# MLP down: the low halves of A21 and A21+A22 from a negative high half by ScalarE and an addition by DMA inside SBUF

## The chip, the cores and the metric

The kernel is one program on 1 core of a Trainium2 chip. The time is the device time of one execution in microseconds (us); a median stands for several runs. The profile is of one execution. Its engines are TensorE (PE, with its weight loads PEld), VectorE (DVE), ScalarE (ACT), GpSimd (POOL) and SyncE (SP). DMAs are issued from the queues of SP, ACT and POOL and moved by 16 DMA engines.

## The reference

Two transformer blocks in float32 on 512 tokens of width 1024. The first is attention with a gated convolution and an MLP; the second has two layers, retention and then chunk attention, each followed by an MLP with a squared ReLU. The change touches only that last MLP, which runs twice:

```python
def _sqrelu_mlp(h, w1, w2):
    u = jax.nn.relu(h @ w1)
    return (u * u) @ w2

for i in range(DEPTH_2):
    ...
    h = h + _sqrelu_mlp(_rmsnorm(h, mlp_norm_g[i]), mlp_w1[i], mlp_w2[i])
```

h is 512x1024, w1 is 1024x4096 and w2 is 4096x1024.

## The kernel before

**Three products for one.** Each float32 operand is split in a high half, rounded to fp32r by ScalarE, and a low half, the operand less the high one. `three` (L1043) multiplies high by high, high by low and low by high. So for each block of weights somebody has to make `w_hi` and then `w_lo`. In the MLPs ScalarE makes the first (`hi_of`, L1756) and VectorE the second (`lo_of`, L3258). GpSimd makes the low halves of most other stages (`lo`, L924).

**The MLP.** It goes in four groups of 1024 hidden columns, `MLP_GROUPS`. In each group the up products come first (units), then seven down products. The down product is a 2x2 block product with seven multiplications, from sums of blocks, in the order A11, A12, S3, M, A21, S1, S4 (`PRODUCTS`, L1516). S1 is A21+A22: its weights are loaded to `raw` and the second block is added by a DMA from HBM (L1016). S3, M and S4 share one buffer, `s3_m_s4` in `aux`: S3 is made by a load and an adding DMA (L1012), M by VectorE, which adds A21 (`m_sum`, L3302), and S4 by a further adding DMA (L1018) once M's low half is made. The hidden blocks are summed in the same way by VectorE: T3, T2, T4 (for A21), T1 (for S1).

**Places.** Every product needs two halves of weights, 128x1024 each. A half is a place (`down`, L174); `w_hi` and `w_lo` have four half slots each, so a half may be written when TensorE is through with the place four before (`released`, L194). Progress is counted in semaphores: `w_hi_ready` by ScalarE, `w_lo_ready` by whoever makes the low half, in the order of the places, `group_done` by TensorE. SyncE loads the next raw weights on `w_lo_ready` (`raw_free`, L220): A21's second half frees the slot of the next group's first weights, S1's that of the second.

**Order around the change.** Each engine runs its list as written. ScalarE: part T4's high half, A21's two high halves, T1's, S1's two, S4's two (L2459 to L2465). VectorE: T4's sum, `take` of a finished product from PSUM, T4's low half, two low halves of A21, T1's sum, a take, T1's low half, two of S1, a take, two of S4, then the takes of Q4 and Q5 (L3477 to L3496). S4 goes into the same PSUM banks as S1, and both results are wanted, S1's alone and the two together, so TensorE waits before each tile of S4 until VectorE has taken Q5 from that tile (L1586). GpSimd: the sums of units, then S3's, S1's and S4's adding DMAs (L1006 to L1018).

Of the kernel before, what the change touches and what calls it, by code (L numbers as in the profile page):

```python
# [348 lines left out]
SEMAPHORES = """first_in0 first_in1 first_in2 first_in3 first_hi rows_in pos_in ident_in kr_in ext_in ext_out bias_in0  # L349
 bias_in1 bias_in2 bias_in3 decay_in tab_in krep_done out_done raw_ready0 raw_ready1 w_hi_ready w_lo_ready group_done  # L350
# [14 lines left out]
def build(nc, T, out):  # L365
# [3 lines left out]
    with ExitStack() as ctx:  # L369
# [359 lines left out]
        def _(sp):  # L729
# [166 lines left out]
            for t in range(4):  # L896
# [850 lines left out]
        def _(act):  # L1747
# [35 lines left out]
            def down_hi(ml, g, b, half):  # L1783
# [536 lines left out]
            def mlp(ml, norm, turned, name, row):  # L2320
# [28 lines left out]
                def plain_squared(m):  # L2349
# [1432 lines left out]
```

## Time and profile before

| | us |
|---|---|
| median of 3 runs | 1985.72 (1985.52 to 1986.9) |
| the profiled execution | 1985.98 |
| its span, first to last instruction | 1984.1 |
| TensorE busy | 1932.1 (97%) |
| VectorE busy | 1324.9 (67%) |
| ScalarE busy | 978.0 (49%) |
| GpSimd busy | 643.7 (32%) |

The mean granted clock of TensorE is 0.994 of full speed. The page gives averages over very different stages; the timeline of one down stage tells more. In a timeline row the first number is the start in us from the span's start, the second the time from the first start to the last end of the merged instructions; a bracket gives the idle time before it and what ended it. Matmuls overlap, so their distance is read from start to start.

### The profile page before, as it was taken

To read this page: it belongs to the slowest core of one execution; us is meant where nothing else is said; L and a number is where in the kernel's file an instruction comes from. 1 tells how busy PE (TensorE), PEld (TensorE's weight loads), DVE (VectorE), ACT (ScalarE), POOL (GpSimd) and SP (SyncE) were. 2 spreads that over 40 slices of the span, in tenths; PEclk is the share of its full clock that TensorE was granted. 3 is DMA by queue.
4 is the path that set the end of the run, shared out by engine and by line. 5 is a ranking of instruction groups with operands and counts; after the bars stand their busy time and mean duration, and the time that the engine had idled before them with its cause. 6 is when DMAs were issued, how large, how long until landed. Compare 5 with 4: busy or idle time off the path is not lost.

```text
span 1984.1 us, 25953 instructions
## 1 busy us (share of the span) xinstructions
PE 1932.1 (97%) x10236; PEld 1643.6 (83%) x10236; DVE 1324.9 (67%) x1807; ACT 978.0 (49%) x1392; POOL 643.7 (32%) x456
## 2 busy tenths in 40 slices
PE   8999999999999999999998999999999998999997
PEld 6877878888888888888887798988888888798896
DVE  7667753432257845454557888889566777888888
ACT  7445442322245442424356564656455556564655
POOL 2333545555455435353542011110333341101010
PEclk9999999999999999999998999999999998999999
DMA  5312367375322322222223556565322233746554
GB/s 162 93 44 75 113 88 122 99 101 115 100 91 85 112 80 93 77 94 75 95 74 106 149 149 170 129 190 135 99 85 84 84 111 81 191 118 188 123 157 127
DMA packets 166220, 221.46 MB, mean 112 GB/s; under 512 B 4512, under 2 KB 119968, under 8 KB 165984
## 3 DMA queue, kind: packets, MB, share of 16 engines
q1 hardware_dynamic: 151600, 190.52, 29.6%
q0 software_dynamic: 12928, 25.71, 7.6%
q10 hardware_dynamic: 1584, 3.74, 4.2%
q8 instruction: 74, 1.21, 0.3%
q14 instruction: 34, 0.28, 0.0%
HBM read 214.84 MB, written 4.72 MB: 111 GB/s over the span
## 4 chain that ended last, share of the span: by engine, by line
PE 65%; DVE 19%; ACT 8%; issue 7%; POOL 1%; DMA 0%; SPq 0%; DVEq 0%; ACTq 0%; POOLq 0%
PE ps L1045 20%; PE ps L1047 20%; PE ps L1046 20%; DVE w_lo L3261 6%; DVE hid_lo L3276 2%; DVE o_buf L3399 2%; ACT w_hi L1759 2%; ACT x L2371 1%; PE ps L1217 1%; PE ps L1247 1%; ACT x L2373 1%; POOL w_lo L929 1%; DVE x L3356 1%; PE ps L1256 1%; ACT hid_hi L2385 1%
## 5 line engine op out<-in xcount | busy, mean ns | idle before, releaser
L929 POOL TENSOR_TENSOR w_lo<-raw,w_hi 128x512 fp32r<-128x512 f32 x376 | 531.8, 1445 | 665.3 <-ACT w_hi L1753 665.3
L1045 PE MATMUL ps<-hn_hi,w_hi 128*128 128x512 f32 (+1 forms) x1524 | 556.5, 365 | 2.2 <-DVE hn_lo L2961 1.7
L1047 PE MATMUL ps<-hn_hi,w_lo 128*128 128x512 f32 (+1 forms) x1524 | 547.7, 359 | 0.0
L1046 PE MATMUL ps<-hn_lo,w_hi 128*128 128x512 f32 (+1 forms) x1524 | 547.6, 359 | 0.0
L1045 PEld LDWEIGHTS ps<-hn_hi,w_hi 128*128 128x128 f32 x1524 | 289.4, 190 | 49.3 <-issue 3.8
L1753 ACT ACTIVATE w_hi<-raw 128x2048 fp32r<-128x2048 f32 (+1 forms) x98 | 186.0, 1898 | 287.1 <-PE ps L1047 287.0
L1047 PEld LDWEIGHTS ps<-hn_hi,w_lo 128*128 128x128 f32 x1524 | 288.8, 190 | 43.1
L1046 PEld LDWEIGHTS ps<-hn_lo,w_hi 128*128 128x128 f32 x1524 | 289.2, 190 | 41.9 <-issue 1.7
L1045 PE MATMUL ps<-w_hi,hid_hi 128*128 128x512 f32 x456 | 180.9, 397 | 22.4 <-issue 9.1
L1046 PE MATMUL ps<-hid_lo,w_hi 128*128 128x512 f32 (+1 forms) x504 | 184.3, 366 | 0.0
L1045 PE MATMUL ps<-hid_hi,w_hi 128*128 128x512 f32 (+1 forms) x488 | 179.5, 368 | 0.0
L1047 PE MATMUL ps<-hid_hi,w_lo 128*128 128x512 f32 (+1 forms) x488 | 178.1, 365 | 0.0
L1047 PE MATMUL ps<-w_hi,hid_lo 128*128 128x512 f32 x456 | 177.8, 390 | 0.0
L1046 PE MATMUL ps<-w_lo,hid_hi 128*128 128x512 f32 x456 | 177.5, 389 | 0.0
L1045 PEld LDWEIGHTS ps<-w_hi,hid_hi 128*128 128x128 f32 x456 | 85.5, 188 | 52.5 <-issue 35.6
L1759 ACT ACTIVATE w_hi<-raw 128x1024 fp32r<-128x1024 f32 x100 | 101.7, 1050 | 51.1 <-PE ps L1047 51.1
L2665 DVE TENSOR_TENSOR scr<-ps,scr 128x512 f32<-128x512 f32 x42 | 27.1, 686 | 138.7 <-PE ps L1047 135.3
L3261 DVE TENSOR_TENSOR w_lo<-raw,w_hi 128x1024 fp32r<-128x1024 f32 x92 | 110.8, 1222 | 7.7 <-ACT w_hi L1759 7.7
L1046 PEld LDWEIGHTS ps<-hid_lo,w_hi 128*128 128x128 f32 x504 | 95.1, 189 | 15.2 <-issue 0.2
L1045 PEld LDWEIGHTS ps<-hid_hi,w_hi 128*128 128x128 f32 x488 | 92.0, 189 | 16.8 <-DVE hid_lo L3061 0.8
L1047 PEld LDWEIGHTS ps<-hid_hi,w_lo 128*128 128x128 f32 x488 | 92.1, 189 | 14.8
L1047 PEld LDWEIGHTS ps<-w_hi,hid_lo 128*128 128x128 f32 x456 | 85.6, 188 | 18.5
(396 smaller groups left out, 3438.6 us busy)
## 6 DMA issues: line engine op xcount, KB each, us to landing
raw<-in_mlp_w SPq DMA_DIRECT2D x50, 1024.0 KB, 5.4
raw<-in_ret_w_in SPq DMA_DIRECT2D x24, 1024.0 KB, 5.1
aux<-in_mlp_w POOLq DMA_DIRECT2D x16, 1024.0 KB, 8.5
unit_raw<-in_mlp_w SPq DMA_DIRECT2D x14, 1024.0 KB, 6.4
raw<-in_att_w_in SPq DMA_DIRECT2D x12, 1024.0 KB, 5.4
raw<-in_w_gate SPq DMA_DIRECT2D x11, 1024.0 KB, 5.3
raw<-in_w_up SPq DMA_DIRECT2D x11, 1024.0 KB, 5.4
raw<-in_w_down SPq DMA_DIRECT2D x8, 1024.0 KB, 8.1
```

Source lines behind the costliest of these rows:

```text
L929: ins = pool.tensor_tensor(w_lo[:, slot, at], raw[:, slot, at], w_hi[:, slot, at].bitcast(F32), ALU.subtract)
L1045: pe.matmul(o, hi, rhs_hi, start=start, stop=False, skip_group_check=True)
L1046: pe.matmul(o, hi, rhs_lo, start=False, stop=False, skip_group_check=True)
L1047: return pe.matmul(o, lo, rhs_hi, start=False, stop=stop, skip_group_check=True)
L1217: ins = pe.matmul(a.score_ps(b, t), q[:, t * P:(t + 1) * P], k[:, 0:(t + 1) * P], start=(n == 0), stop=(n == last), skip_group_check=True)
L1247: ins = pe.transpose(a.trans_ps(b, j)[:, (t - j) * P:(t - j + 1) * P], a.score_sb(b, t)[:, j * P:(j + 1) * P], ident[:, :])
L1753: act.activation(w_hi[:, c.slot, 0:columns], raw[:, c.slot, 0:columns], ACT.Copy)\
L1759: act.activation(half_slot(w_hi, ml, place), src, ACT.Copy).then_inc(s["w_hi_ready"], ml.step(place))
L2665: dve.tensor_tensor(dst, ps[:, g.bank(m), :], r, ALU.mult).then_inc(pair_free[g.pair], 1)
L3261: dve.tensor_tensor(half_slot(w_lo, ml, place), src, half_slot(w_hi, ml, place).bitcast(F32), ALU.subtract)\
L3276: dve.tensor_tensor(lo_part, p_block(block), hi_part.bitcast(F32), ALU.subtract).then_inc(s["mlp_lo"], 1)
L3399: ins = dve.scalar_tensor_tensor(o, ps[:, bank + n, :], r_two[:, at:at + 1], o, ALU.mult, ALU.add)
```

## The change

In every group of both MLPs the four low halves of A21 and S1 are made otherwise. ScalarE writes the negative of the rounded block to the slot in `w_lo`, then the high half to `w_hi` as before. GpSimd issues a DMA from `raw` to `w_lo` with addition, which leaves raw less high. When it has landed GpSimd counts `w_lo_ready` up. VectorE drops these four subtractions and waits for S1's before it makes S4's. Several semaphores are put together: `m_summed` goes into `mlp_sum`, `out_done` and `ext_out` into `rows_out`.

```diff
+    BY_DMA = (A21, S1)
...
+    def by_dma(self, g, b):
+
+        return (2 * (self.first + g) + self.BY_DMA.index(b) + 1) * 16
...
     def first_sums(self, n):
-        return 20 * self.layer + n
+        return 28 * self.layer + n
 
     def sums(self, g, n):
-        return 20 * self.layer + 4 + 4 * g + n
+        return 28 * self.layer + 4 + 6 * g + n
...
-SUM = {T3: 1, T2: 2, T4: 3, T1: 4}
+SUM = {T3: 1, T2: 2, T4: 5, T1: 6}
+FIRST_SUM = {T3: 1, T2: 2, T4: 3, T1: 4}
+M_HALF = (3, 4)
...
+            def low_added(ml, g, b):
+
+                for half, landed in enumerate(("lo_first_in", "lo_second_in")):
+                    place = ml.down(g, b, half)
+                    pool.wait_ge(s["w_hi_ready"], ml.ready(place))
+                    pool.dma_start(half_slot(w_lo, ml, place), down_source(ml, g, b, half), accum_op=ALU.add)\
+                        .then_inc(s[landed], 16)
+
+            def low_landed(ml, g, b):
+
+                for half, landed in enumerate(("lo_first_in", "lo_second_in")):
+                    pool.wait_ge(s[landed], ml.by_dma(g, b))
+                    pool.nop().then_inc(s["w_lo_ready"], 1)
+
...
                     pool.dma_start(s1, w2[g, 0, 1], accum_op=ALU.add).then_inc(s["s1_added"], 16)
+                    low_added(ml, g, ml.A21)
                     pool.wait_ge(s["w_lo_ready"], ml.ready(ml.down(g, ml.M, 1)))
                     pool.dma_start(s3, w2[g, 0, 0], accum_op=ALU.add).then_inc(s["s4_added"], 16)
+                    low_landed(ml, g, ml.A21)
+                    low_added(ml, g, ml.S1)
+                    low_landed(ml, g, ml.S1)
...
+                if b in ml.BY_DMA:
+                    place = ml.down(g, b, half)
+                    act.wait_ge(s["group_done"], ml.released(place))
+                    act.activation(half_slot(w_lo, ml, place), down_source(ml, g, b, half), ACT.Copy, scale=-1.0)
                 hi_of(ml, ml.down(g, b, half), down_source(ml, g, b, half))
...
                     part_lo(g, T4)
-                    down_lo(g, ml.A21, 0)
-                    down_lo(g, ml.A21, 1)
                     t1(g)
                     take(g, ml.Q6, ml.M, 1, 1, 0, X, ALU.subtract)
                     part_lo(g, T1)
-                    down_lo(g, ml.S1, 0)
-                    down_lo(g, ml.S1, 1)
                     take(g, ml.Q2, ml.A11, 1, 0, 0, Z, ALU.add)
+                    dve.wait_ge(s["w_lo_ready"], ml.ready(ml.down(g, ml.S1, 1)))
                     down_lo(g, ml.S4, 0)
```

Three places of the order of instructions show it, all of group 1 of the first MLP but for GpSimd's, which are of group 0; the groups are alike. In the names, the tile written stands before the arrow. Lines of the changed kernel are some 7 to 29 higher.

ScalarE before, from M's high halves to S4's (L1759 makes a high half, L2385 that of a hidden part):

```order
L1759 ACTIVATE w_hi<-aux 128x1024 [waits group_done,m_summed] x2
L2385 ACTIVATE hid_hi<-x 128x1024 [waits mlp_sum]
L1759 ACTIVATE w_hi<-raw 128x1024 [waits group_done,raw_ready0] x2
L2385 ACTIVATE hid_hi<-x 128x1024 [waits mlp_sum]
L1759 ACTIVATE w_hi<-raw 128x1024 [waits group_done,s1_added] x2
L1759 ACTIVATE w_hi<-aux 128x1024 [waits group_done,s4_added] x2
```

and in the change (L1784 and L2414 are these two, L1824 the negative copy):

```order
L1784 ACTIVATE w_hi<-aux 128x1024 [waits group_done,mlp_sum] x2
L2414 ACTIVATE hid_hi<-x 128x1024 [waits mlp_sum]
L1824 ACTIVATE w_lo<-raw 128x1024 [waits group_done,raw_ready0]
L1784 ACTIVATE w_hi<-raw 128x1024 [waits group_done]
L1824 ACTIVATE w_lo<-raw 128x1024 [waits group_done,raw_ready0]
L1784 ACTIVATE w_hi<-raw 128x1024 [waits group_done]
L2414 ACTIVATE hid_hi<-x 128x1024 [waits mlp_sum]
L1824 ACTIVATE w_lo<-raw 128x1024 [waits group_done,s1_added]
L1784 ACTIVATE w_hi<-raw 128x1024 [waits group_done]
L1824 ACTIVATE w_lo<-raw 128x1024 [waits group_done,s1_added]
L1784 ACTIVATE w_hi<-raw 128x1024 [waits group_done]
L1784 ACTIVATE w_hi<-aux 128x1024 [waits group_done,s4_added] x2
```

Each high half of A21 and S1 has a negative copy in front of it, and T4's and T1's high halves (`hid_hi`) stand where they stood.

GpSimd before: the adding DMAs to S3, S1 and S4, then the next unit's sum:

```order
L1012 DMA aux<-in_mlp_w_2 128x4x512 [waits s3_in]
L1016 DMA raw<-in_mlp_w_2 128x4x512 [waits raw_ready1]
L1018 DMA aux<-in_mlp_w_2 128x4x512 [waits w_lo_ready]
L1001 TENSOR_TENSOR raw<-raw 128x1024 [waits unit_summed]
```

and in the change (an instruction that only waits and counts has no row; its waits are shown with the next one):

```order
L1033 DMA aux<-in_mlp_w_2 128x4x512 [waits s3_in]
L1037 DMA raw<-in_mlp_w_2 128x4x512 [waits raw_ready1]
L1015 DMA w_lo<-raw 128x1024 [waits w_hi_ready] x2
L1040 DMA aux<-in_mlp_w_2 128x4x512 [waits w_lo_ready]
L1015 DMA w_lo<-raw 128x1024 [waits lo_first_in,lo_second_in,w_hi_ready]
L1015 DMA w_lo<-raw 128x1024 [waits w_hi_ready]
L1008 TENSOR_TENSOR raw<-raw 128x1024 [waits lo_first_in,lo_second_in,unit_summed]
```

A21's two DMAs stand before S4's. S1's stand behind S4's and behind the waits for A21 to land; the next unit's sum stands behind S1's landing.

VectorE before, from T4's low half to the takes of Q4 (L3261 is a low half of weights, L3276 of a hidden part, L3399 a take):

```order
L3276 TENSOR_TENSOR hid_lo<-x,hid_hi 128x1024 [waits mlp_hi]
L3261 TENSOR_TENSOR w_lo<-raw,w_hi 128x1024 [waits w_hi_ready] x2
L3299 SCALAR_TENSOR_TENSOR x<-x 128x4x256 [waits mlp_lo,mlp_sum]
L3399 SCALAR_TENSOR_TENSOR o_buf<-ps,r_two,o_buf 128x512 [waits mlp_taken,group_done]
L3399 SCALAR_TENSOR_TENSOR o_buf<-ps,r_two,o_buf 128x512
L3276 TENSOR_TENSOR hid_lo<-x,hid_hi 128x1024 [waits mlp_hi]
L3261 TENSOR_TENSOR w_lo<-raw,w_hi 128x1024 [waits w_hi_ready] x2
L3399 SCALAR_TENSOR_TENSOR o_buf<-ps,r_two,o_buf 128x512 [waits mlp_taken,group_done]
L3399 SCALAR_TENSOR_TENSOR o_buf<-ps,r_two,o_buf 128x512
L3261 TENSOR_TENSOR w_lo<-aux,w_hi 128x1024 [waits w_hi_ready] x2
L3399 SCALAR_TENSOR_TENSOR o_buf<-ps,r_two,o_buf 128x512 [waits mlp_taken,group_done]
L3399 SCALAR_TENSOR_TENSOR o_buf<-ps,r_two,o_buf 128x512
```

and in the change (L3290, L3305 and L3428):

```order
L3305 TENSOR_TENSOR hid_lo<-x,hid_hi 128x1024 [waits mlp_hi]
L3328 SCALAR_TENSOR_TENSOR x<-x 128x4x256 [waits mlp_lo,mlp_sum]
L3428 SCALAR_TENSOR_TENSOR o_buf<-ps,r_two,o_buf 128x512 [waits mlp_taken,group_done]
L3428 SCALAR_TENSOR_TENSOR o_buf<-ps,r_two,o_buf 128x512
L3305 TENSOR_TENSOR hid_lo<-x,hid_hi 128x1024 [waits mlp_hi]
L3428 SCALAR_TENSOR_TENSOR o_buf<-ps,r_two,o_buf 128x512 [waits mlp_taken,group_done]
L3428 SCALAR_TENSOR_TENSOR o_buf<-ps,r_two,o_buf 128x512
L3290 TENSOR_TENSOR w_lo<-aux,w_hi 128x1024 [waits w_hi_ready,w_lo_ready]
L3290 TENSOR_TENSOR w_lo<-aux,w_hi 128x1024 [waits w_hi_ready]
L3428 SCALAR_TENSOR_TENSOR o_buf<-ps,r_two,o_buf 128x512 [waits mlp_taken,group_done]
```

Two pairs of low halves are gone, and the first one of S4 waits for `w_lo_ready` too, with the takes behind it.

## Rows read from the trace of the kernel before

**Rows 1.** Waits of TensorE: engine and line, releaser: us in total, times, longest.
```profile
PE ps L1045 <- issue: 9.1, 8, 1.2
PE ps L1045 <- DVE w_lo L3261: 8.9, 15, 1.5
```

**Rows 2.** Timeline, TensorE, group 1: start, us, operation, [idle before, releaser].
```profile
1203.25 0.39 PE L1047 MATMUL ps<-w_hi,hid_lo 128*128 128x512 f32 x1
1204.41 0.47 PE L1045 MATMUL ps<-w_hi,hid_hi 128*128 128x512 f32 x1 [0.77 <-DVE w_lo L3261]
...
1209.71 0.39 PE L1047 MATMUL ps<-w_hi,hid_lo 128*128 128x512 f32 x1
1210.27 0.47 PE L1045 MATMUL ps<-w_hi,hid_hi 128*128 128x512 f32 x1 [0.17 <-DVE w_lo L3261]
...
1221.46 0.39 PE L1047 MATMUL ps<-w_hi,hid_lo 128*128 128x512 f32 x1
1222.98 0.47 PE L1045 MATMUL ps<-w_hi,hid_hi 128*128 128x512 f32 x1 [1.13 <-issue]
```

**Rows 3.** Timeline, VectorE, the same stretch.
```profile
1203.04 2.36 DVE L3261 TENSOR_TENSOR w_lo<-aux,w_hi 128x1024 fp32r<-128x1024 f32 x2
...
1206.45 1.41 DVE L3399 SCALAR_TENSOR_TENSOR o_buf<-ps,r_two,o_buf 128x512 f32<-128x512 f32 x2
1207.77 1.22 DVE L3276 TENSOR_TENSOR hid_lo<-x,hid_hi 128x1024 fp32r<-128x1024 f32 x1
1208.90 2.36 DVE L3261 TENSOR_TENSOR w_lo<-raw,w_hi 128x1024 fp32r<-128x1024 f32 x2
...
1217.03 1.41 DVE L3399 SCALAR_TENSOR_TENSOR o_buf<-ps,r_two,o_buf 128x512 f32<-128x512 f32 x2
1218.35 2.36 DVE L3261 TENSOR_TENSOR w_lo<-aux,w_hi 128x1024 fp32r<-128x1024 f32 x2
1220.61 3.12 DVE L3399 SCALAR_TENSOR_TENSOR o_buf<-ps,r_two,o_buf 128x512 f32<-128x512 f32 x4
```

**Rows 4.** Timeline, ScalarE, the same stretch.
```profile
1206.57 1.06 ACT L2385 ACTIVATE hid_hi<-x 128x1024 fp32r<-128x1024 f32 x1 [4.79 <-DVE x L3293]
1207.54 1.99 ACT L1759 ACTIVATE w_hi<-raw 128x1024 fp32r<-128x1024 f32 x2
```

**Rows 5.** Timeline, GpSimd, the same stretch.
```profile
1196.47 1.28 POOL L1016 DMA_DIRECT2D raw<-in_mlp_w  x1 [30.14 <-DMA raw<-in_mlp_w]
1205.69 1.28 POOL L1018 DMA_DIRECT2D aux<-in_mlp_w  x1 [7.94 <-DVE w_lo L3261]
```

**Rows 6.** DMA issues: out<-in, queue, count, KB each, us from issue to landing.
```profile
raw<-in_mlp_w SPq DMA_DIRECT2D x50, 1024.0 KB, 5.4
...
aux<-in_mlp_w POOLq DMA_DIRECT2D x16, 1024.0 KB, 8.5
...
raw<-in_mlp_w POOLq DMA_DIRECT2D x8, 1024.0 KB, 8.4
...
hid_hi<-hid_hi SPq DMA_DIRECT2D x3, 64.0 KB, 2.0
```

**Rows 7.** Windows: us, busy PE PEld DVE ACT POOL, PEclk, DMA share, GB/s.
```profile
1197.00:1198.00 1.00, 1.00 (x6) 0.84 (x5) 1.00 (x2) 0.00 (x0) 0.75 (x1) 1.00 0.00 0
1198.00:1199.00 1.00, 1.00 (x6) 0.81 (x6) 1.00 (x2) 0.75 (x1) 0.00 (x0) 1.00 0.54 41
...
1203.00:1204.00 1.00, 0.64 (x3) 0.19 (x1) 1.00 (x2) 0.00 (x0) 0.00 (x0) 1.00 1.15 211
1204.00:1205.00 1.00, 0.59 (x3) 0.54 (x4) 1.00 (x2) 0.00 (x0) 0.00 (x0) 1.00 0.28 47
```

**Rows 8.** Timeline, SyncE's queue, group 1: the load of the next group's weights.
```profile
1211.29 0.37 SPq L832 DMA_DIRECT2D raw<-in_mlp_w  x1
```

**Rows 9.** Timeline, TensorE, start of the first MLP, after a wait of 5.50 us.
```profile
1069.09 1.12 PE L1608 MATMUL ps<-ident,x 128*128 128x128 f32 x4 [5.50 <-ACT o_buf L2325]
...
1072.98 0.63 PE L1045 MATMUL ps<-hn_hi,w_hi 128*128 128x512 f32 x1
1073.41 0.63 PE L1046 MATMUL ps<-hn_lo,w_hi 128*128 128x512 f32 x1
```

**Rows 10.** Windows, the same stretch: columns as in the windows above.
```profile
1068.00:1072.00 4.00, 2.92 (x13) 2.92 (x14) 4.00 (x5) 3.97 (x7) 0.00 (x0) 0.50 0.00 0
```

More of the change, by code:

```diff
@@ L347 @@
 N_MLPB = Norm(N_ATT, 8, 12, columns=True)
-SEMAPHORES = """first_in0 first_in1 first_in2 first_in3 first_hi rows_in pos_in ident_in kr_in ext_in ext_out bias_in0
- bias_in1 bias_in2 bias_in3 decay_in tab_in krep_done out_done raw_ready0 raw_ready1 w_hi_ready w_lo_ready group_done
+SEMAPHORES = """first_in0 first_in1 first_in2 first_in3 first_hi rows_in pos_in ident_in kr_in ext_in rows_out bias_in0
+ bias_in1 bias_in2 bias_in3 decay_in tab_in krep_done raw_ready0 raw_ready1 w_hi_ready w_lo_ready group_done
  pair_free0 pair_free1 memset_done gains_t gains_ready x_t x_copied p_t p_hi p_lo
@@ L884, in _ @@
                 if j == 1:
-                    sp.wait_ge(s["ext_out"], H2 * 16)
+                    sp.wait_ge(s["rows_out"], H2 * 16)
                     sp.wait_ge(s["mask_set"], 4)
@@ L901, in _ @@
                     sp.wait_ge(s["fin_right"], t - 1)
-                sp.dma_start(out[0, t * P:(t + 1) * P, :], y_tok[:, t, :]).then_inc(s["out_done"], 16)
-            sp.wait_ge(s["out_done"], 64)
+                sp.dma_start(out[0, t * P:(t + 1) * P, :], y_tok[:, t, :]).then_inc(s["rows_out"], 16)
+            sp.wait_ge(s["rows_out"], H2 * 16 + 64)
         @block.gpsimd
@@ L1787, in down_hi @@
                 elif b == ml.M:
-                    act.wait_ge(s["m_summed"], 2 * (ml.first + g) + half + 1)
+                    act.wait_ge(s["mlp_sum"], ml.sums(g, M_HALF[half]))
                 elif b == ml.S1:
@@ L2134, in spread_ext @@
                 act.dma_start(ext_rows[n], ext[n:n + 1, :].unsqueeze(1).to_broadcast([1, 64, EXT]))\
-                    .then_inc(s["ext_out"], 16)
+                    .then_inc(s["rows_out"], 16)
             def gate_up(ph, i, g_hid, pairs, first=False):
@@ L2353, in plain_squared @@
                     act.wait_ge(s["x_t"], turned + 2 * m + 2)
-                    act.wait_ge(s["mlp_sum"], ml.first_sums(SUM[T4]))
+                    act.wait_ge(s["mlp_sum"], ml.first_sums(FIRST_SUM[T4]))
                     act.activation(u, ps[:, bank:bank + 2, :], ACT.Relu).then_inc(s["mlp_up_taken"], 1)
@@ L2389, in first_group @@
                     gained_b12()
-                    act.wait_ge(s["mlp_sum"], ml.first_sums(SUM[T3]))
+                    act.wait_ge(s["mlp_sum"], ml.first_sums(FIRST_SUM[T3]))
                     first_t(T3, t3_raw)
@@ L2393, in first_group @@
                     unit_hi(ml, 0, 1, ml.U_A12)
-                    act.wait_ge(s["mlp_sum"], ml.first_sums(SUM[T2]))
+                    act.wait_ge(s["mlp_sum"], ml.first_sums(FIRST_SUM[T2]))
                     first_t(T2, t2_raw, -1.0)
-                    act.wait_ge(s["mlp_sum"], ml.first_sums(SUM[T1]))
+                    act.wait_ge(s["mlp_sum"], ml.first_sums(FIRST_SUM[T1]))
                     act.wait_ge(s["norm_acc"], norm.acc0 + norm.added)
@@ L3307, in m_sum @@
                     s3 = down_source(ml, g, ml.S3, half)
-                    dve.tensor_tensor(s3, s3, down_source(ml, g, ml.A21, half), ALU.add).then_inc(s["m_summed"], 1)
+                    dve.tensor_tensor(s3, s3, down_source(ml, g, ml.A21, half), ALU.add).then_inc(s["mlp_sum"], 1)
                 def unit_s3_sum(g, u):
@@ L3364, in first_sums @@
                     ins.then_inc(s["mlp_sum"], 1)
-                    dve.wait_ge(s["mlp_sum"], ml.first_sums(SUM[T3]))
+                    dve.wait_ge(s["mlp_sum"], ml.first_sums(FIRST_SUM[T3]))
                     for k in range(4):
@@ L3369, in first_sums @@
                     ins.then_inc(s["mlp_sum"], 1)
-                    dve.wait_ge(s["mlp_sum"], ml.first_sums(SUM[T2]))
+                    dve.wait_ge(s["mlp_sum"], ml.first_sums(FIRST_SUM[T2]))
                     for k in range(4):
```

4 lines of the change are left out of this document (2 added, 2 removed).

## The prediction

> **What bounds the kernel now.** Read the list of who waited for whom first, for TensorE [rows 1]. It is small: 8.9 us in 15 waits for VectorE's low halves (L3261), and 9.1 us in 8 waits of about 1.1 us that the profile calls issue. There are eight down stages (four groups in each of two MLPs), so a wait that comes 8 times comes once in each of them. Then the timeline of one such stage, group 1 of the first MLP. The other seven look the same there, within 0.1 us.
>
> TensorE [rows 2]: the product M starts at 1204.41 and its last matmul at 1209.71, so 24 matmuls come (1209.71 - 1204.41) / 23 = 0.23 us apart and a product takes 5.5 us. At each product's start there is more than 0.23 us between two starts: 1.16 before M, 0.56 before A21 (S1 has the same), 1.52 before S4. The excess is 0.93, 0.33, 0.33 and 1.29 us. VectorE explains it [rows 3]: from 1203.04 on it has no gap. Per product it does a token sum, a two-tile take, a part's low half and two weight halves: from the start of M's halves (1203.04) to the start of A21's (1208.90) that is 5.86 us, against TensorE's 5.5. S4 is the last link: S1's take of Q2 at 1217.03, the two halves of S4 at 1218.35, then takes of Q4 and Q5 at 1220.61, of which S4 needs the first half of Q5. So in this stage VectorE is the slower engine, and what lies behind M is worth 0.33 + 0.33 + 1.29 = 1.95 us a stage, 15.6 us in all, 0.8%. That is all that taking work from VectorE can give here.
>
> **The change, part by part.** It takes four VectorE subtractions out of a stage, 32 in all, at 1.14 us each (2.36 for a pair) [rows 3]; 36 us of busy time, of which at most the 15.6 us above were on the path. It adds 32 ScalarE copies (1.99 for a pair, so about 0.95 us each) [rows 4], 32 DMAs of 512 KB inside SBUF with addition, and their waits on GpSimd. The semaphores that share a counter or a name cost nothing: the order of the counts is unchanged, and none adds an instruction.
>
> ScalarE, A21. It stood idle before A21, so its time is not the question, its place is. T4's high half runs at 1206.57 and the copies of A21 follow it at once, at 1207.54 [rows 4]. In the new order each half is two activations: minus the high half at 1207.5, the high half at 1208.5, done 1209.5; the second half done at 1211.4. In the kernel before VectorE then needed 1.2 us per half and A21 began at 1210.27 [rows 2].
>
> The DMA. The trace has no addition from SBUF to SBUF, but it has the same addition from HBM: 1024 KB, issued by GpSimd, 1.28 us on GpSimd and 8.4 to 8.5 us from issue to landing [rows 5, 6]. The one issued at 1196.47 moves nothing before 1198.5 or so, runs at about 205 GB/s with the DMA engines fully busy, and is over at 1204.3 [rows 5, 7]: 2.0 us before data, 5.75 us of data, 0.6 us after. For 512 KB I take half the data time: 2.0 + 2.9 + 0.6 = 5.5 us. The nearest cheaper rows are plain copies: 1024 KB in 5.4 us and, inside SBUF, 64 KB in 2.0 us [rows 6]. On the line through these two 512 KB land in 3.6 us, with 1.6 us of data. The dear end is that an addition from SBUF takes for 512 KB the data time of the 1024 KB, 5.75 us. I take the middle one, since it is the same operation on the same queue.
>
> The sum, with the times of group 1. A21's first half: hi ready 1209.6, lands 1215.1. TensorE, which ended M at 1209.9, waits 5.2 us where it waited 0.3. A21's second half is issued at 1211.45 and its data goes behind the first's, 1214.5 to 1217.4, landed 1218.0. On GpSimd the 1024 KB addition for S4 now stands behind these two issues: it was issued at 1205.69 [rows 5], now at 1212.75, and on the one GpSimd queue its data runs 1217.4 to 1223.1. Next GpSimd waits for A21 to land before it may issue S1, though S1's high halves are ready by 1214.2 and 1216.2 (T1's high half at 1211.4, then four activations of 0.95). So S1's DMAs are issued at 1218.1 and 1219.4, and their data goes behind S4's: 1226.0 and 1228.9, landed 1226.6 and 1229.5. The chain of data is without a hole from 1211.6 on: 2.9 + 2.9 + 5.75 + 2.9 + 2.9 = 17.35 us, which is why ready times matter less than the rate.
>
> VectorE waits for S1's second landing before S4's halves, and behind that wait stand the two halves, the take of Q4 and that of Q5, all of which S4 needs: 2.27 + 1.31 + 0.75 + 0.15 for the semaphore is 4.5 us, so S4 starts at 1234.1 in place of 1222.98: 11.1 us later. TensorE's own work from 1229.5 is 6 + 12 matmuls of 0.23, 4.1 us, just hidden by that. What the change was to remove (1.95 us a stage) is inside this sum: nothing of it is left.
>
> Two additions. First, the load of the next group's first weights is released by A21's second low half. Before, it was issued at 1211.29 [rows 8]; now at 1218.1, in the middle of the chain of additions. A plain 1024 KB keeps the engines busy for about 2.9 us (5.4 less some 2.5 of latency). If it takes its full share, S1 lands 2.9 us later; if it fits beside the additions, nothing. I take 1.4. The Trainium skill, page "DMA: Bandwidth & Descriptors", section "SWDGE vs HWDGE vs iDMA", says that an engine takes GpSimd's and the other queues in turn; no row here shows an addition and a load over a full length, and by it the full 2.9 would be paid. Second, the clock. After 5.5 us of idle TensorE the granted clock was 0.50 (1.2 GHz), and its 128x512 matmuls came 0.43 us apart in place of 0.23 [rows 9, 10]. A21's wait is as long. A21 has 5.9 us of cover (it ends at 1220.7, S1 comes at 1226.6), so its slow matmuls are free; S1's 18 remaining ones would be 7.7 us against VectorE's 4.5, at most 3.2 more. I take 0.5, since the wait before S1 may be short of what lowers the clock.
>
> 11.1 + 1.4 + 0.5 = 13.0 us a stage, eight stages: 104 us. The profiled execution took 1985.98 (span 1984.1), the median is 1985.72, so I forecast **2090 us**, 5% slower. The stages do not help each other: each ends with S4 on VectorE, and the next group's first halves follow it as now. The second load of the next group waits for S1's landing and comes about 1 us later against S4's start than now; it is wanted only 8 us after that start.
>
> **Rivals.**
> *Plain prices (2010 to 2060).* If an addition inside SBUF costs what a plain copy does, A21 lands at 1213.2 and 1215.1, S4's addition (still HBM, 5.75 of data) ends at 1220.6, S1's at 1224.4, and S4 starts at 1229.0: 6.0 us a stage, 2034. For it: the source is near. Against it: the additions seen keep the engines full at about 205 GB/s, so they are bound by the adding and not by HBM.
> *Slow adding (over 2130).* With 5.75 us of data per 512 KB the chain ends 11.5 us later and S4 starts 22.6 us late: 181 us, 2167. With the full share of the load and a cold S1 at my rates: 11.1 + 2.9 + 3.2 = 17.2 a stage, 2123.
> *No queueing (2015).* The DMAs land 3.6 us after their issue, as on the line of the plain rows, and don't hold one another up: A21 at 1213.2 and 1215.1, S1's second half (issued 1216.5) at 1220.1. Then S4's own addition is last, issued at 1212.75 in place of 1205.69 and landed 8.4 us later, 1221.2; high halves, low halves and two takes behind it put S4 at 1226.7, 3.7 us late: 30 us. The Trainium skill, the same page, section "Anatomy of one DMA", is near this: it fits a GpSimd DMA as 2.0 us plus its bytes over 436 GB/s, so 3.2 us for 512 KB and 4.4 us for 1024 KB, estimates from that page. For an addition the trace disagrees: 8.4 us for 1024 KB [rows 6].
> *Not slower (1970).* VectorE's order is freed and the landings are hidden: 15.6 us gained. It needs A21's first low half within 0.4 us of its high half (1209.5 against 1209.9) and S1's within what VectorE's four takes give back. The issue alone is 1.28 us on GpSimd, so this needs ScalarE's copies of A21 to run before T4's high half, and the order of rows says they don't. It decides at a landing of 0.4 us; I see none under 2.0.
> *The change doesn't do what it says.* VectorE would still make these halves. Its new order has no such row for A21 or S1, so this has no chance.
>
> **How the numbers follow.** Forecast (the addition at the rate seen, 2060 to 2130): 0.53. Plain prices: 0.2. No queueing: 0.05. Slow adding or both extras in full: 0.18. Not slower: 0.02, within 0.2%: 0.02. The range leaves out no queueing, the not slower cases, and the outer part of the slow one: 2030 to 2150. A measurement of this kernel tells about 0.2% from no change: faster 0.02, same 0.02, slower 0.96.
>
> **What would show it.** In the changed profile: DMAs of 512 KB from raw to w_lo, 5.5 us alone and over 8 us for S1's when queued; TensorE idle about 5 us before A21 and about 5 more in two pieces in S1, released by a DMA or by GpSimd; S4's wait put to VectorE; each down stage near 54 us long in place of 41; VectorE idle some 13 us in it, before L3290; the clock at 0.5 in parts of A21. I am wrong if S4's addition does not hold back S1's, if 512 KB land in under 4 us, or if TensorE's slow clock shows outside A21.

## The result, and the profile after

The changed kernel takes 2092.89 us (median of 4, 2092.45 to 2096.25) against 1986.31 us for the kernel before (median of 4, 1985.52 to 1987.01): a ratio of 1.0540, 95% interval 1.0523 to 1.0557. That is 107 us slower, where 104 were forecast. The profiled execution took 2092.45 us with a span of 2090.7, and the mean granted clock is 0.970, before 0.994.

First the page of the changed kernel: busy time of each engine, and of its DMA issues the two that bear on the change (out<-in, queue, count, KB each, median us from issue to landing).

```profile
PE 1966.2 (94%) x10236; PEld 1668.8 (80%) x10236; DVE 1293.1 (62%) x1775; ACT 1007.6 (48%) x1424; POOL 671.8 (32%) x488
...
aux<-in_mlp_w POOLq DMA_DIRECT2D x16, 1024.0 KB, 9.5
w_lo<-raw POOLq DMA_DIRECT2D x32, 512.0 KB, 7.1
```

VectorE lost 1324.9 - 1293.1 = 32 us of work, ScalarE gained 30. The 32 DMAs are there, and S4's addition takes 9.5 us where the same kind took 8.5 [rows 6]. TensorE's busy time rose by 34 us with the same 10236 matmuls: they ran at the low clock in part. Next, who waited for whom, TensorE (us in total, times, longest).

```profile
PE ps L1070 <- POOLq L1022: 83.5, 16, 6.8
...
PE ps L1070 <- DVE w_lo L3290: 8.4, 8, 1.5
```

L1022 is GpSimd's count after a landing, so this is A21 and S1 in eight down stages. The eight issue waits of [rows 1] are gone, since TensorE now comes to S4 late anyway. Now the timeline of group 1 as in [rows 2 to 5]; M starts at 1218.29. First TensorE's rows with a wait, and VectorE.

```profile
1218.29 0.47 PE L1070 MATMUL ps<-w_hi,hid_hi 128*128 128x512 f32 x1 [0.84 <-DVE w_lo L3290]
1228.45 0.76 PE L1070 MATMUL ps<-w_hi,hid_hi 128*128 128x512 f32 x1 [4.47 <-POOLq L1022]
1242.92 0.77 PE L1070 MATMUL ps<-w_hi,hid_hi 128*128 128x512 f32 x1 [6.21 <-POOLq L1022]
```
```profile
1227.41 1.41 DVE L3428 SCALAR_TENSOR_TENSOR o_buf<-ps,r_two,o_buf 128x512 f32<-128x512 f32 x2
1245.48 2.36 DVE L3290 TENSOR_TENSOR w_lo<-aux,w_hi 128x1024 fp32r<-128x1024 f32 x2 [16.66 <-POOLq L1022]
1247.76 2.26 DVE L3428 SCALAR_TENSOR_TENSOR o_buf<-ps,r_two,o_buf 128x512 f32<-128x512 f32 x3
```

A21 begins 10.2 us after M (before 5.9), S1 24.6 (before 11.7), and S4, at 1250.68, 32.4 (before 18.6). VectorE, which had no gap here, stands for 16.7 us. Then ScalarE up to A21's last half, GpSimd, and SyncE's queue with the load of the next group's first weights, issued as the first of the two rows merged here.

```profile
1220.44 1.06 ACT L2414 ACTIVATE hid_hi<-x 128x1024 fp32r<-128x1024 f32 x1 [4.80 <-DVE x L3322]
1221.41 1.04 ACT L1824 ACTIVATE w_lo<-raw 128x1024 fp32r<-128x1024 f32 x1
...
1224.25 1.04 ACT L1784 ACTIVATE w_hi<-raw 128x1024 fp32r<-128x1024 f32 x1
```
```profile
1223.70 0.89 POOL L1015 DMA_DIRECT2D w_lo<-raw  x1 [12.04 <-ACT w_hi L1784]
1225.59 0.86 POOL L1015 DMA_DIRECT2D w_lo<-raw  x1 [1.00 <-ACT w_hi L1784]
1226.14 1.64 POOL L1040 DMA_DIRECT2D aux<-in_mlp_w  x1
1232.92 1.76 POOL L1015 DMA_DIRECT2D w_lo<-raw  x2 [5.14 <-DMA w_lo<-raw]
```
```profile
1232.42 13.43 SPq L839 DMA_DIRECT2D raw<-in_mlp_w  x2
```

The order is the forecast one: A21's two DMAs, S4's addition, and only after A21's landing S1's two. The first addition, issued at 1223.70 with nothing ahead of it, lands 4.6 us later; S4's, issued at 1226.14, lands after 11.4; S1's two after 9.8 and 11.9. The windows of the changed kernel show what the data did (us, busy PE PEld DVE ACT POOL, granted clock, DMA share, GB/s).

```profile
1226.00:1227.00 1.00, 0.00 (x0) 0.00 (x0) 0.73 (x1) 1.00 (x2) 1.00 (x2) 1.00 1.04 197
...
1230.00:1231.00 1.00, 1.00 (x4) 0.81 (x3) 0.00 (x0) 0.03 (x1) 0.00 (x0) 0.50 1.19 123
...
1234.00:1235.00 1.00, 1.00 (x6) 0.79 (x5) 0.00 (x0) 0.00 (x0) 0.68 (x1) 1.00 1.13 203
...
1238.00:1239.00 1.00, 0.00 (x0) 0.00 (x0) 0.00 (x0) 1.00 (x2) 0.00 (x0) 1.00 1.08 382
...
1242.00:1243.00 1.00, 0.08 (x1) 0.11 (x1) 0.00 (x0) 0.00 (x0) 0.00 (x0) 0.50 1.04 210
```

From 1225 to 1244 the DMA engines are full (windows of 1 us with a share of 0.97 or more, but for 0.71 in the one from 1231). Additions move about 200 GB/s, as before [rows 7], except for A21's second one, in whose last 2 us the rate falls to 117 to 123; for nearly 3 us in the middle the rate is 382. The list of DMA queues says whose data that is (queue: packets, MB, share of the 16 engines): q0 is GpSimd's with the additions, q1 the one with the plain loads. Of 1232 to 1236, and of 1237 to 1239:

```profile
q0 software_dynamic: 403, 0.82, 112.8%
```
```profile
q1 hardware_dynamic: 750, 0.77, 108.6%
q0 software_dynamic: 3, 0.00, 0.1%
```

The load, issued at 1232.42, moves nothing while S4's addition runs; then it runs alone, and S1's additions, issued half a microsecond after it, stand. Only its last 0.05 MB come beside them, between 1240 and 1245.

### The profile page after: what moved, and what is told of

The parts are those of the page before. It is cut to its first block, busy times and chain, and to the rows that moved or that the text cites. A ratio compares the mean times of both kernels' runs of the same rounds, so it can differ in the third digit from the quotient of the medians.

```text
span 2090.7 us, 26025 instructions
## 1 busy us (share of the span) xinstructions
PE 1966.2 (94%) x10236; PEld 1668.8 (80%) x10236; DVE 1293.1 (62%) x1775; ACT 1007.6 (48%) x1424; POOL 671.8 (32%) x488
## 3 DMA queue, kind: packets, MB, share of 16 engines
q8 instruction: 74, 1.21, 0.2%
## 4 chain that ended last, share of the span: by engine, by line
PE 66%; DVE 14%; ACT 7%; DMA 6%; issue 5%; POOL 1%; SPq 0%; DVEq 0%; POOLq 0%; ACTq 0%
PE ps L1070 21%; PE ps L1071 20%; PE ps L1072 20%; DMA w_lo<-raw 6%; DVE w_lo L3290 4%; ACT x L2400 1%; ACT w_hi L1784 1%; PE ps L1242 1%; ACT x L2402 1%; PE ps L1272 1%; DVE hid_lo L3305 1%; POOL w_lo L936 1%; DVE x L3385 1%; ACT hid_hi L2414 1%; PE ps L1281 1%
## 5 line engine op out<-in xcount | busy, mean ns | idle before, releaser
L1070 PE MATMUL ps<-w_hi,hid_hi 128*128 128x512 f32 x456 | 195.7, 429 | 95.1 <-POOLq L1022 83.5
L1070 PEld LDWEIGHTS ps<-w_hi,hid_hi 128*128 128x128 f32 x456 | 94.2, 206 | 127.3 <-issue 105.2
L1071 PE MATMUL ps<-w_lo,hid_hi 128*128 128x512 f32 x456 | 191.2, 419 | 0.0
L1072 PE MATMUL ps<-w_hi,hid_lo 128*128 128x512 f32 x456 | 189.9, 416 | 0.0
L1784 ACT ACTIVATE w_hi<-raw 128x1024 fp32r<-128x1024 f32 x100 | 102.9, 1048 | 90.0 <-PE ps L1072 90.0
L3290 DVE TENSOR_TENSOR w_lo<-aux,w_hi 128x1024 fp32r<-128x1024 f32 x48 | 57.2, 1220 | 129.3 <-POOLq L1022 129.3
L2694 DVE TENSOR_TENSOR scr<-ps,scr 128x512 f32<-128x512 f32 x42 | 27.1, 686 | 138.7 <-PE ps L1072 135.3
L1072 PEld LDWEIGHTS ps<-w_hi,hid_lo 128*128 128x128 f32 x456 | 93.8, 206 | 21.7
L1071 PEld LDWEIGHTS ps<-w_lo,hid_hi 128*128 128x128 f32 x456 | 94.6, 207 | 18.8
L1070 PEld LDWEIGHTS ps<-hid_hi,w_hi 128*128 128x128 f32 x488 | 92.1, 189 | 16.7 <-DVE hid_lo L3090 0.8
```

The lines of the kernel that those rows point to most:

```text
L1070: pe.matmul(o, hi, rhs_hi, start=start, stop=False, skip_group_check=True)
L1071: pe.matmul(o, hi, rhs_lo, start=False, stop=False, skip_group_check=True)
L1072: return pe.matmul(o, lo, rhs_hi, start=False, stop=stop, skip_group_check=True)
L1784: act.activation(half_slot(w_hi, ml, place), src, ACT.Copy).then_inc(s["w_hi_ready"], ml.step(place))
L2694: dve.tensor_tensor(dst, ps[:, g.bank(m), :], r, ALU.mult).then_inc(pair_free[g.pair], 1)
L3290: dve.tensor_tensor(half_slot(w_lo, ml, place), src, half_slot(w_hi, ml, place).bitcast(F32), ALU.subtract)\
```

## The experiments

Each is compared with the kernel before, run beside it on the same chip. Times after M are those of group 1 unless another stage is named.

**1. Each block alone.** A21 alone by DMA, S1's halves back on VectorE:

```diff
-    BY_DMA = (A21, S1)
+    BY_DMA = (A21,)
...
+                    down_lo(g, ml.S1, 0)
+                    down_lo(g, ml.S1, 1)
```

In this run VectorE also waits for A21's count before it makes S1's halves, since the places are counted in order.

> Only A21's low halves are made by the DMA, S1's by VectorE as before. All times are from M's start in a stage, where S4 started at 18.6 us in the kernel before and at 32.4 us in the changed one. Theory (one chain of additions on GpSimd's queue, here A21, A21, S4's own, lands as in the changed kernel): A21 starts at 10.2 us, S4's addition lands at 19.2, its high and low halves and two takes put S4's start at 24.6, 6.0 us late, 8 stages: about 2035 us, with TensorE waiting once for GpSimd's count in a stage, 4.5 us. Rival (the two products cost the same each, the sum is 13.3 us a stage): half of the loss, 2040 us, but then with A21's start late by 6.7 us. Rival (only the wait for A21 of 4.5 us counts, S4's delayed addition is hidden): 4.3 us a stage, 2021 us.

Measured: 2038.48 us, ratio 1.0264 (1.0247 to 1.0281); A21 at +10.2, S1 +17.9, S4 +25.1. The theory held within 4 us. The first rival's time, 2040, is as near, but it needed A21 6.7 us late, and A21 is 4.3 us late. And S1 alone by DMA:

```diff
-    BY_DMA = (A21, S1)
+    BY_DMA = (S1,)
...
+                    down_lo(g, ml.A21, 0)
+                    down_lo(g, ml.A21, 1)
```

> Only S1's low halves are made by the DMA, A21's by VectorE. Theory (chain of additions): S4's own addition is issued and lands as in the kernel before, S1's first half lands 15.5 us after M's start, the second 18.0, so S1 starts at 15.6 in place of 11.7 and S4 at 22.9 in place of 18.6: 4.3 us a stage, 2021 us. With the loss of this run and that of the run with A21 alone summing to less than the 106 us of both (35 + 49 = 84), since in the changed kernel S1's DMAs also stand behind A21's and beside the load. Rival (they add up plainly): 2092 - 49 = 2043 us.

Measured: 2031.58 us, 1.0227 (1.0210 to 1.0244); S1 at +16.3, S4 at +23.6 in group 1 and up to +25.0 in the other stages. That is 10 us over the theory and 12 under the rival. The losses are 52 and 45 us, 97 together, against 107 for both: nearly additive, and not the 84 of the theory. Each block pays for its own landing, and the rest comes when they queue.

**2. The transfers left out.** GpSimd's waits and counts stay; the DMAs are gone. A21's counts are also moved behind S4's adding DMA, which is issued as early as in the kernel before.

```diff
-                    pool.dma_start(half_slot(w_lo, ml, place), down_source(ml, g, b, half), accum_op=ALU.add)\
-                        .then_inc(s[landed], 16)
+                    pool.nop().then_inc(s[landed], 16)
```

> The DMAs inside SBUF are left out: ScalarE still writes the negative copy and GpSimd still counts up when the high half is ready, so w_lo of A21 and S1 holds minus the high half, and part of the result is not computed. It measures the change without its transfers. Theory (the loss is all in the transfers and their order; ScalarE's 32 copies are hidden and VectorE is relieved): S4 starts about 17.3 us after M in place of 18.6, A21 and S1 without a wait: 1.3 us a stage gained, 1976 us. Rival (ScalarE's list is a bound by itself, the copies delay T1's and S1's high halves): 1986 us or more, TensorE waiting in S1.

Measured: 1985.53 us, 0.9992 (0.9983 to 1.0002), not the 1976 expected. The timeline shows why: A21 is at +7.3, since the first half is counted only after the second is ready, and TensorE waits 12.7 us for that count in 8 times. The edit put this wait there, so the question was asked again with each half counted by itself.

```diff
-                    pool.wait_ge(s[landed], ml.by_dma(g, b))
+                    pool.wait_ge(s["w_hi_ready"], ml.ready(ml.down(g, b, half)))
```

> The run without DMAs again (the additions are left out, so part of the result is not computed), but GpSimd counts each half up as soon as its own high half is ready. In the first such run it counted both halves of a product only after the second one, and A21 started at 7.30 us after M in place of 5.86, which was the edit's doing. Theory (the loss is all in the transfers): A21 starts at 5.4 to 5.6 us, S1 at 11.1, S4 near 17 in place of 18.57: 1.6 us a stage gained, about 1973 us. Rival (the longer ScalarE list costs what VectorE gives back): 1984 to 1988 us, with S1 waiting for its second half.

Measured: 1978.25 us, 0.9959 (0.9943 to 0.9974). A21 +5.5, S1 +11.0, S4 +17.4, and of TensorE's waits for S4 0.86 us are left (waits, then timeline of this kernel):

```profile
PE ps L1069 <- issue: 6.8, 8, 0.9
```
```profile
1220.80 0.47 PE L1069 MATMUL ps<-w_hi,hid_hi 128*128 128x512 f32 x1 [0.86 <-issue]
```

So with transfers that cost nothing the change would have given 8 us, half of the 15.6 that the prediction called the most there is. The DMAs, with their issue on GpSimd, the later addition for S4 and the waits for landings, cost those 8 us and the 107 on top. From M to M of the next group it is 80.6 us here, before 81.7: the gain of the stage stays.

**3. The adding.** The same DMAs as plain copies of the same size; the addition is left out of the computation.

```diff
-                    pool.dma_start(half_slot(w_lo, ml, place), down_source(ml, g, b, half), accum_op=ALU.add)\
+                    pool.dma_start(half_slot(w_lo, ml, place), down_source(ml, g, b, half))\
```

> The 32 DMAs from raw to w_lo are plain copies and don't add, so the low halves are wrong and part of the result is not computed; their size, queue and order stay. Theory (the adding sets the rate, 5.4 us of data per 1024 KB against 2.9 for a plain load): A21 starts 9.3 us after M, the chain ends 5 us earlier, S4 starts at 27.3 in place of 32.3: about 2053 us. Rival (GpSimd's queue or the copying inside SBUF sets the rate): no change, 2092 us.

Measured: 2054.95 us, 1.0337 (1.0321 to 1.0353), within 2 us of what was expected. The page of this kernel has the copies at

```profile
w_lo<-raw POOLq DMA_DIRECT2D x32, 512.0 KB, 5.0
```

where the additions had 7.1. With nothing ahead one lands in 2.9 us, where the addition took 4.6. A21 comes at +8.5 in place of +10.2, S4 at +25.7 in group 1 and at +26.9 on average (27.3 expected). The adding is worth 38 of the 107 us, and plain copies on this path would still cost 69. The windows (columns as before) show a copy of A21 and then S4's addition, which is unchanged here:

```profile
1222.00:1223.00 1.00, 0.92 (x2) 0.83 (x3) 1.00 (x2) 1.00 (x2) 0.76 (x1) 0.50 1.12 410
...
1226.00:1227.00 1.00, 1.00 (x6) 0.79 (x6) 0.00 (x0) 0.00 (x0) 0.13 (x1) 1.00 1.13 205
```

This run also shows how the plain load goes with other work. Issued at 1223.9, it moves nothing while S4's addition runs, as in the changed kernel; from 1225 to 1228 the queue list has q0 alone, 112.0%. But beside S1's plain copies it does move (queue list of 1229 to 1233):

```profile
q0 software_dynamic: 328, 1.09, 80.7%
q1 hardware_dynamic: 329, 0.34, 30.1%
```

As many packets of the one as of the other, 328 and 329: the queues take turns. So it is beside additions that the load and GpSimd's DMAs hardly mix.

**4. The load of the next group.** Released only by S1's second half:

```diff
-            return self.ready(self.down(g - 1, (self.A21, self.S1)[j], 1))
+            return self.ready(self.down(g - 1, self.S1, 1))
```

> The changed kernel, but the load of the next group's first weights waits for S1's low halves in place of A21's, so it no longer runs beside the additions. Theory (the 1024 KB load takes its full share of the DMA engines from the chain; in the last group, which has no such load, S4's low halves started 23.8 us after M and not 27.2): 3.0 us a stage gained in 7 stages, about 2071 us, S1's landings 3 us earlier. Rival (GpSimd's queue and the adding bound the chain, the load fits beside it): 2092 us, no change. Rival (the later load becomes a new wait before the next group's up products): over 2092 us.

Measured: 2080.45 us, 1.0474 (1.0456 to 1.0491): 12 us of the expected 21. In the stages the gain is there: S1 at +21.8 in place of +24.6, VectorE's halves for S4 from +24.2 in place of +27.1, and S4 earlier by 21 us in the seven stages together (in group 1 at +28.8 in place of +32.4). But the load is late for the next up products, and TensorE waits there, for a sum that VectorE makes later (waits of this kernel):

```profile
PE ps L1070 <- DVE x L3369: 4.8, 6, 1.2
```

That is 4.8 of the 9 us given back; the rest was not taken apart. The last stage of the changed kernel says the same without an edit, for no load follows it: S1 +21.4, S4 +28.6.

**5. The order of the additions.** S4's is issued ahead of A21's, as early as before.

```diff
-                    low_added(ml, g, ml.A21)
                     pool.wait_ge(s["w_lo_ready"], ml.ready(ml.down(g, ml.M, 1)))
                     pool.dma_start(s3, w2[g, 0, 0], accum_op=ALU.add).then_inc(s["s4_added"], 16)
+                    low_added(ml, g, ml.A21)
```

> The changed kernel, but GpSimd issues S4's own addition before A21's DMAs, where it stood in the kernel before. Theory (one queue in order, so what stands between A21's and S1's additions delays S1): S4's addition lands at 9.7 us after M as before, A21 starts later (12.4 in place of 10.2), S1's second half lands at 24 in place of 27.2, S4 starts near 28.9 in place of 32.3: 3.4 us a stage gained, about 2065 us. Rival (the sum of the data counts, not its order): 2092 us.

Measured: 2090.28 us, 1.0526 (1.0510 to 1.0542). The order is worth 3 us, not 28, and the two intervals overlap. What A21 loses (+12.4) S1 doesn't win back (+24.2), and TensorE's waits stay (first the waits of this kernel, then its timeline):

```profile
PE ps L1070 <- POOLq L1022: 85.3, 16, 7.4
```
```profile
1230.52 0.77 PE L1070 MATMUL ps<-w_hi,hid_hi 128*128 128x512 f32 x1 [6.68 <-POOLq L1022]
1242.30 0.76 PE L1070 MATMUL ps<-w_hi,hid_hi 128*128 128x512 f32 x1 [4.50 <-POOLq L1022]
```

The rival's time held, but its reason, that the sum of the data decides, is not the whole of it. That sum is 3.15 MB at 205 GB/s, 15.4 us, and the load's 3. Here the data starts nearly 4 us earlier (after 1221, with M at 1218.13) and ends less than 1 us earlier, because there is a hole in it (windows of this kernel):

```profile
1232.00:1233.00 1.00, 1.00 (x4) 0.81 (x3) 0.00 (x0) 0.00 (x0) 0.00 (x0) 0.50 0.15 25
1233.00:1234.00 1.00, 1.00 (x4) 0.78 (x4) 0.00 (x0) 0.00 (x0) 0.61 (x2) 0.55 0.04 6
```

GpSimd issues S1's DMAs only when A21's have landed (+15.3), and the load, issued 0.5 us before them, goes first, from 1234 to 1239. S1's second half lands at +26.5, in the changed kernel at +27.1. In the last stage, without a load, it lands at +23.1, near the 24 of the theory. What the theory left out is the load. No run has both this order and the later load.

**6. GpSimd makes low halves by arithmetic.** From the kernel before, in search of a version that takes work from VectorE without a transfer: GpSimd subtracts the second halves of A21 and S1.

```diff
+                pool.tensor_tensor(half_slot(w_lo, ml, place), down_source(ml, g, b, 1),
+                                   half_slot(w_hi, ml, place).bitcast(F32), ALU.subtract).then_inc(s["w_lo_ready"], 1)
...
+                    second_low(ml, g, ml.A21)
+                    second_low(ml, g, ml.S1)
```

> The kernel before, with VectorE relieved in another way: GpSimd makes the second low half of A21 and of S1 by a subtraction of its own (in place of idling), VectorE the first, and ScalarE makes S1's high halves before T1's. No DMA is added. Theory (behind M the stage is bound by VectorE, 5.86 us a product against 5.5 on TensorE, and 1.95 us a stage are to be had): A21 starts at 5.5 us after M, S1 at 11.0, S4 at 16.6 in place of 5.86, 11.72, 18.57: 1.9 us a stage, 1971 us. Rival (GpSimd's subtraction of 128x1024, 2.4 us alone and 3.3 us beside VectorE, comes too late for the product's second part): TensorE waits inside A21 or S1 and the gain is under half, 1980 us or more.

Measured: 1986.07 us, 1.0000 (0.9991 to 1.0009). A21 stays at +5.9 and S4 at +18.5, S1 comes at +12.0, and TensorE waits 5.7 us in 16 times for GpSimd's halves. Then M's second half as well:

```diff
+                    second_low(ml, g, ml.M)
```

> The kernel before with the second low halves of M, A21 and S1 made by GpSimd's subtraction (M's is new against the run with two), each started when its high half is ready, and S1's high halves before T1's on ScalarE. In the run with two, A21 still started at 5.86 us after M, since M's second half stood on VectorE ahead of A21's first; S1 came late (12.03) since GpSimd waited for the first half. Theory (what counts is which of VectorE's steps stand ahead of each product's first half): A21 at 5.5, S1 at 11.0, S4 at 16.6 to 17 us: 1.7 to 1.95 us a stage gained, 1971 to 1973 us. Rival (GpSimd beside VectorE slows both, or TensorE waits for a second half): 1980 us or more.

Measured: 2009.23 us, 1.0106 (1.0089 to 1.0123). And S3's too:

```diff
+                    second_low(ml, g, ml.S3)
```

> As the run with three, and S3's second low half is GpSimd's too, with VectorE's take of Q1 moved ahead of its second sum for M. Theory (the wait of 0.93 us before M has the same cause): M starts 5.5 us after S3 in place of 6.4, 0.9 us a stage more, 1964 to 1966 us. Rival (S3's second half, 3.3 us on GpSimd, delays the second sum for M and so M's second half, or holds back the addition for S1 on GpSimd's list): no better than the run with three.

Measured: 2013.54 us, 1.0135 (1.0118 to 1.0152), and its rival, no better than the run with three, held. All three missed by 15 to 49 us, and the timeline of the second shows two reasons. GpSimd takes 2.4 us or more for a half that takes VectorE 1.14, and that half is now on the path (TensorE waits 31.4 us in 16 times for GpSimd's counts; M alone comes 8.6 us after S3, before 6.4, which is 17 of the 22 us lost). And VectorE's operations grow where GpSimd's run. VectorE, then GpSimd, of the kernel with three halves on GpSimd:

```profile
1206.00 3.41 DVE L3293 TENSOR_TENSOR hid_lo<-x,hid_hi 128x1024 fp32r<-128x1024 f32 x1
...
1212.92 1.21 DVE L3293 TENSOR_TENSOR hid_lo<-x,hid_hi 128x1024 fp32r<-128x1024 f32 x1
...
1215.19 3.42 DVE L3316 SCALAR_TENSOR_TENSOR x<-x 128x1024 f32<-128x1024 f32 x1
...
1220.17 2.59 DVE L3293 TENSOR_TENSOR hid_lo<-x,hid_hi 128x1024 fp32r<-128x1024 f32 x1 [0.24 <-ACT hid_hi L2400]
```
```profile
1205.95 2.38 POOL L1007 TENSOR_TENSOR w_lo<-aux,w_hi 128x1024 fp32r<-128x1024 f32 x1 [4.08 <-ACT w_hi L1774]
...
1214.76 2.77 POOL L1007 TENSOR_TENSOR w_lo<-raw,w_hi 128x1024 fp32r<-128x1024 f32 x1 [2.34 <-ACT w_hi L1774]
1219.27 2.41 POOL L1007 TENSOR_TENSOR w_lo<-raw,w_hi 128x1024 fp32r<-128x1024 f32 x1 [1.74 <-ACT w_hi L1774]
```

Alone VectorE takes 1.21 us. Each of the three that start while GpSimd's runs ends 1.08 us after GpSimd's end (1209.41 against 1208.33, 1218.61 against 1217.53, 1222.76 against 1221.68): the end of its work waits for GpSimd's. The takes, which read one block from PSUM and one from SBUF, are not longer beside GpSimd: 1.41 us at 1211.75 in the kernel with two halves, while GpSimd subtracts from 1210.85 to 1214.10. The Trainium skill, page "SBUF — State Buffer", section "SBUF: two separate sides", says that the two engines share a pair of ports as "an exclusive lock, not a bandwidth split", held for a whole instruction, for VectorE operations with two SBUF inputs too. These rows agree.

**7. The order of VectorE's sums.** Experiment 2 had shown that S4's last 0.86 us are not a matter of low halves. Before, VectorE adds up A21's two tiles, then S1's, and S4 needs only S1's [rows 3]. From the kernel before:

```diff
-                    take(g, ml.Q4, ml.A21, 1, 1, 0, Y, ALU.add)
...
                     take(g, ml.Q5 + 1, ml.S1, 1, 1, 1, X, ALU.subtract, slice(1, 2))
+                    take(g, ml.Q4, ml.A21, 1, 1, 0, Y, ALU.add)
```

> The kernel before, with one thing moved: VectorE adds up S1's two token tiles (each 0.68 to 0.78 us) ahead of A21's two (together 1.31 us), where A21's stood first; every wait on how many sums are done is renumbered to match. No low half, DMA or product moves. In the kernel before S4's products start 18.57 us after M's, 1.13 to 1.29 us after S1's last product has been issued, and VectorE is the one waited for: it ends S4's low halves, then adds up A21 (1.31 us), then S1's first tile, and only that last one is needed by S4. THEORY (what is left of TensorE's wait in the stage is the order of VectorE's sums, not the time that the low halves take, which is why both the DMA form and GpSimd's help could never gain more than about 1.1 us a stage): S4 starts at about +17.3 to +17.5 after M, the wait is gone, 8 stages by 1.1 = 9 us, 1977 us (0.9955). RIVAL 1 (the gain is given back in the next group: VectorE's low halves and sums for the next up products are no earlier, so TensorE reaches them 1.1 us sooner and waits there): 1985 us, ratio 1.000, with new waits behind the next group's first units. RIVAL 2 (S1's second tile isn't done when VectorE comes to it, and what stands behind it is held): S4's start +17.5 but its second tile late, 1981 us.

Measured: 1987.51 us (median of 11), 1.0003 (0.9994 to 1.0012). In the stage the theory held: S4 at +17.3 in place of +18.6. Rival 1 held outside it. First two rows of TensorE's waits in this kernel, then one of its timeline, 15 us after S4's start.

```profile
PE ps L1045 <- DVE w_lo L3261: 9.4, 16, 1.5
...
PE ps L1045 <- DVE x L3340: 4.9, 6, 1.1
```
```profile
1235.43 0.39 PE L1045 MATMUL ps<-t_hi_t,w_hi 128*128 128x256 f32 x1 [0.76 <-DVE x L3340]
```

The 9.1 us of issue waits are gone; 4.9 come back for a sum in the next up products, and from M to M of the next group it is 81.5 us, before 81.7. In experiment 2, where VectorE had less work and not only another order, it was 80.6. Where the last part of the gain went was not taken apart.

## Why the prediction was right, point by point

- **What bounds the stage.** That the stage is VectorE's held: without transfers TensorE's waits fell (experiment 2). That 15.6 us were to be had did not. S4's 1.29 us was counted as low halves' time, but of the 1.95 us a stage only 1.13 came with free transfers, for S4 still waits for VectorE, 0.86 us. An earlier S4 alone is given back in the next group (experiment 7). This step put the gain too high, and nothing of the forecast hung on it.
- **ScalarE's place.** Copies of A21 at 1207.5 to 1211.4 forecast against T4's high half at 1206.57; measured 0.97 to 4.85 us after the same row. Held.
- **The price of the addition.** Forecast 5.5 us for 512 KB; measured 4.6 us with nothing ahead. The term was 0.9 too dear: the data took 2.65 us (1225.15 to 1227.8) and not 2.9, and the rest of a landing 2.0, not 2.6. A21's second half, at the lower rate, took 3.4 us of data, so that part of the error was given back. A21 came at +10.2, forecast +10.9. That the adding sets the rate, and not HBM or the distance, was right (experiment 3).
- **The queue.** S4's addition behind A21's, S1's behind S4's: held in the rows, and S4's landing after 11.4 us as forecast (1212.75 to 1223.7, 11.0). Experiment 5 shows that another order alone gains almost nothing while S1 waits for A21's landing and for the load.
- **The load.** Forecast 1.4 us, bounds 0 to 2.9. Measured: VectorE's halves for S4 start 27.1 to 27.2 us after M in the seven stages with a load, and 24.2 us after it when the load is held back (experiment 4). So the load costs 2.9 us, the upper bound. This is the term that was mis-sized most. The last stage, which has no load, gives 3.3 by the same row (+23.8), but there A21's second half lands 0.8 us earlier too. Beside additions the load doesn't share the engines: it waits for the one that runs and then goes nearly whole before the next. The rule of taking queues in turn, that the prediction named from the Trainium skill, page "DMA: Bandwidth & Descriptors", section "SWDGE vs HWDGE vs iDMA", is not what the queue list shows beside additions: 112.8% and nothing, then 108.6% and 0.1%. Beside plain copies it is, 328 packets against 329 (experiment 3). The price that the prediction took from that rule, the full share, was the right one all the same. The kernel before had a hint: its load was issued at 1211.29 [rows 8], S4's addition ran to 1213.5, and in the queue list of 1211 to 1213 q0 stands alone, 113.0%.
- **The clock.** Forecast 0.5 us a stage. The granted clock fell to 0.50 in both waits of TensorE: windows of 1 us have 0.54 from 1227, 0.50 from 1228 to 1233, then 0.86 from 1240 and 0.50 from 1241 to 1247. A21's slow matmuls are hidden. In S1 VectorE has S4's last need done at 1250.02, and TensorE starts S4 at 1250.68 without a wait: 0.66 us after it, before 0.10, so some 0.5 us is the slow matmuls' part. The size held. That "the wait before S1 may be short" was wrong, it was 6.21 us, and a slow clock outside A21, which the prediction had named as a sign of being wrong, did show: S1's first ten matmuls are 0.43 us apart.
- **The sum.** Forecast 11.1 + 1.4 + 0.5 = 13.0 us a stage. Measured 10.2 + 2.9 + 0.5 = 13.6: the chain by experiment 4 (VectorE's halves at +24.2, the forecast had them at +25.2), then the load, then the clock. By stage S4 is 13.4 to 13.8 us late seven times and 10.0 once, together 105.7 us. The chain was forecast 7 us too dear in all. The load was 9 us too cheap, though it was counted in eight stages and the last has none. That the total came within 3 us is luck in so far as these two nearly cancel.
- **The rivals.** Plain prices gave 2034, or 6.0 us a stage, with no load in it; with real plain copies it is 8.6 a stage, 2055. Slow adding fell: the data of 512 KB took 2.65 us and, at the lower rate, 3.4, not 5.75. No queueing fell, and not slower fell at its own point: the landing was 4.6 us, and it needed 0.4.

## What to carry to other kernels

Before work is moved from a compute engine to a DMA, set the landing time against the slack of the consumer, not the busy time against the busy time: here 1.14 us on VectorE became 4.6 us of landing, where the prediction had found 0.4 us of slack for A21. Then add up all the data that will be in flight in that stretch, loads included and in full, each kind at its own rate. Another order alone moved the wait and gained 3 of the 107 us. And a wait that ends on VectorE is not worth its length until it is known what VectorE does in the next stage.

## What was new about the hardware

- An addition by DMA inside SBUF runs at the same 200 or so GB/s as one from HBM, at full DMA engines, while plain copies inside SBUF on the same queue reached 410 GB/s (experiment 3) and a plain load 382. From 1230 to 1232 A21's second addition moved only 117 to 123 GB/s, with the addition from HBM issued behind it; in experiment 5, with none behind it, the same two additions ran at 201 to 221. Why is open.
- A plain load issued while a GpSimd addition ran did not move until that was over, and then held up the additions issued after it for 3 us. Beside plain copies on GpSimd's queue it took turns with them (experiment 3). No run here tells what makes additions different, nor whether the order of issue would decide between a load and an addition that both stand ready.
- A VectorE operation with two SBUF inputs that starts while a GpSimd subtraction runs ends 1.08 us after it: 3.4 us in place of 1.2. One with a single SBUF input beside PSUM was not longer.
